# First norm of a two-block transformer kernel: x turned as it lands, roots applied behind the projections

## The reference, cut to what matters

```python
def rms_norm(x, g):
    x32 = x.astype(jnp.float32)
    y = x32 * lax.rsqrt(jnp.mean(x32 * x32, axis=-1, keepdims=True) + EPS)
    return (y * g.astype(jnp.float32)).astype(x.dtype)

h = rms_norm(x, mix_pre_g[0])
qkv = h @ w_qkv
q, k, v = jnp.split(qkv, [1024, 2048], axis=-1)
q, k = apply_partial_rope(q, cos, sin), apply_partial_rope(k, cos, sin)
# then softmax attention of two halves per head, and the rest of both blocks
```

## Time and profile before

| | |
|---|---|
| median of 3 executions | 1638.26 us (1637.98 to 1638.42) |
| span of the profiled execution, first to last instruction | 1637.0 us |
| what lies around the span (the median less the span) | 1.26 us |
| TensorE busy (matmul) | 1607.3 us, 98% |
| TensorE weight loads busy | 1406.3 us, 86% |
| VectorE busy | 1035.9 us, 63% |
| ScalarE busy | 826.8 us, 51% |
| Pool busy | 149.0 us, 9% |
| mean granted TensorE clock | 0.997 |

### The profile page before, as it was taken

One profiled execution on the slowest core, in us unless ns is written; L12 is line 12 of the kernel. 1 busy time (PEld: TensorE's weight loads), 2 busy tenths in 40 slices (PEclk: granted clock), 3 DMA queues, 4 the chain that ended last, 5 costly groups with the idle time before them and its releaser, 6 DMA issues.

```text
span 1637.0 us, 24195 instructions
## 1 busy us (share of the span) xinstructions
PE 1607.3 (98%) x10033; PEld 1406.3 (86%) x10033; DVE 1035.9 (63%) x1708; ACT 826.8 (51%) x1191; POOL 149.0 (9%) x141
## 2 busy tenths in 40 slices
PE   7999999999999999999999999999999999999997
PEld 6888888887889988888899999889888888789986
DVE  5686766655645577766665667567747876655554
ACT  4565544443669854444454564444545546354442
POOL 1220010100012200101001100001000000001000
PEclk9999999999999999999999999999999999999999
DMA  9756866777663355555555576598572564575552
GB/s 324 248 192 233 270 211 230 250 249 245 217 207 109 124 190 183 190 196 206 182 179 180 181 157 184 175 196 164 141 153 67 132 171 165 180 250 179 180 191 77
DMA packets 224412, 309.37 MB, mean 189 GB/s; under 512 B 5004, under 2 KB 146720, under 8 KB 224304
## 3 DMA queue, kind: packets, MB, share of 16 engines
q1 hardware_dynamic: 222208, 301.55, 60.2%
q0 software_dynamic: 1664, 5.84, 1.0%
q10 hardware_dynamic: 432, 0.45, 0.1%
HBM read 306.77 MB, written 1.05 MB: 188 GB/s over the span
## 4 chain that ended last, share of the span: by engine, by line
PE 89%; DVE 6%; ACT 3%; issue 1%; DMA 0%; ACTq 0%; DVEq 0%
PE ps L144 86%; PE ps L147 2%; DVE wl L157 2%; DVE SM L167 1%; DVE MT L167 1%; ACT L153 1%; ACT wh L153 1%; ACT SA L153 1%; DVE X L167 0%; ACT FT L153 0%; DVE MT L164 0%; DMA X<-in_x_dram 0%; DVE SM L163 0%; DVE SA L167 0%; ACT YF L153 0%
## 5 line engine op out<-in xcount | busy, mean ns | idle before, releaser
L157 DVE TENSOR_TENSOR wl<-raw,wh 128x1024 fp32r<-128x1024 f32 x498 | 607.8, 1260 | 381.0 <-ACT wh L153 380.3
L144 PE MATMUL ps<-XT,wh 128*128 128x256 f32 (+1 forms) x2880 | 642.2, 311 | 3.0 <-issue 2.2
L153 ACT ACTIVATE wh<-raw 128x1024 fp32r<-128x1024 f32 x498 | 501.5, 1052 | 204.6 <-PE ps L144 114.1
L144 PEld LDWEIGHTS ps<-XT,wh 128*128 128x128 f32 x2880 | 468.2, 189 | 47.3 <-issue 13.6
L144 PE MATMUL ps<-XT,wl 128*128 128x256 f32 x1792 | 502.7, 280 | 0.6 <-DVE wl L157 0.6
L144 PEld LDWEIGHTS ps<-XT,wl 128*128 128x128 f32 x1792 | 337.8, 189 | 1.3 <-DVE wl L157 1.0
L144 PE MATMUL ps<-wh,XT 128*128 128x512 f32 x704 | 224.8, 400 | 0.0
L144 PEld LDWEIGHTS ps<-wh,XT 128*128 128x128 f32 x704 | 131.3, 188 | 32.3 <-issue 1.0
L144 PE MATMUL ps<-wl,XT 128*128 128x512 f32 x352 | 139.0, 395 | 0.0
L144 PE MATMUL ps<-wh,HTH 128*128 128x512 f32 x352 | 137.4, 390 | 0.0
L144 PE MATMUL ps<-wl,HTH 128*128 128x512 f32 x352 | 137.1, 389 | 0.0
(11 more groups left out here) (293 smaller groups left out, 1740.4 us busy)
## 6 DMA issues: line engine op xcount, KB each, us to landing
raw<-in_w_ffn_in_dram SPq DMA_DIRECT2D x66, 1024.0 KB, 5.2
raw<-in_ffn_w_gate_up_dram SPq DMA_DIRECT2D x44, 1024.0 KB, 5.1
raw<-in_w_in_dram SPq DMA_DIRECT2D x40, 1024.0 KB, 8.5
raw<-in_w_ada_dram SPq DMA_DIRECT2D x36, 1024.0 KB, 5.6
raw<-in_w_ffn_out_dram SPq DMA_DIRECT2D x30, 1024.0 KB, 5.0
raw<-in_ffn_w_down_dram SPq DMA_DIRECT2D x20, 1024.0 KB, 5.0
raw<-in_a_w_qkv_dram SPq DMA_DIRECT2D x12, 1024.0 KB, 7.4
raw<-in_kv_w_dram SPq DMA_DIRECT2D x8, 1024.0 KB, 5.5
```

The lines of the kernel that those rows point to most:

```text
L144: return NOTHING if self.e is None else self.e.matmul(o, l, r, start=start, stop=stop, skip_group_check=skip)
L153: return self.e.activation(o, i, fn, bias=bias, scale=scale)
L157: return NOTHING if self.e is None else self.e.tensor_tensor(o, a, b, f)
```

## The change

- TensorE transposes x itself, as soon as x and the identity have landed, not the scaled copy OA, which is no longer made.
- On VectorE, XTL moves from step 1 to step 0, behind the first sum of squares. The roots move to step 1, and are followed by two multiplications of the identity by the roots of the two token tiles (128x128 each, tile DG).
- Before the first rotation TensorE multiplies a matrix of ones by these two diagonals (`root_row`, one float32 matmul of 256 columns): a row of roots on every partition. It takes a PSUM bank and gives it back. VectorE multiplies both tables by it, once; VectorE's and Pool's rotations wait for this.
- ScalarE evicts the first block's values with a scale per token instead of none.

```diff
@@ tensor program
+            def root_row():
+                o = take("r0")
+                pe.wait_ge(*d_cst.at())
+                pe.wait_ge(*v_small.at("r0"))
+                pe.mm(o[:, 0:T], con("one"), DG[:, 0:T], True, True).then_inc(*p_small.up("r0"))
+                give(("r0",), v_small, "turns")
             def rotate(i):
+                if i == TURNS[0]:
+                    root_row()
                 o = take("rot", i)
...
-                to_halves("h0", blocks_of(OA), lambda t, k: v_norm.at("n0", t))
+                to_halves("h0", blocks_of(X), lambda t, k: d_x.at("x"))
@@ ScalarE, rows_out(name, dst, roots=None)
+                    by = 1.0
+                    if roots is not None:
+                        act.wait_ge(*v_norm.at("n0", "r"))
+                        by = roots[:, t:t + 1]
+                    act.act(dst[:, t, n0:n0 + 512], ps(name, t, n0)[:, :], ACT.Copy, 0.0, by).then_inc(
...
-                values, tick = rows(8, rows_out("av", VA)), iter(A_TICKS)
+                values, tick = rows(8, rows_out("av", VA, small(S_MAIN + 8, 2))), iter(A_TICKS)
@@ VectorE, rotate
+                if q == 0:
+                    dve.wait_ge(*p_small.at("r0"))
+                    dve.tt(two(GB[:, 0:2 * T]), two(GB[:, 0:2 * T]), ps("r0")[:, 0:T].unsqueeze(1).to_broadcast([P, 2, T]),
+                           ALU.mult).then_inc(*v_small.up("turns"))
+                    dve.wait_ge(*v_small.at("turns"))
@@ VectorE, main
                 next_after(dve.dot(small(S_MAIN, 1), OA[:, 0, :], X[:, 0, :], X[:, 0, :]))
+                dve.wait_ge(*d_vec.at("vec"))
+                to_halves("h0", XTH, XTL, gain("mix_pre_g"))
+                yield
                 dve.wait_ge(*a_norm.at("n0", "sq"))
                 rstd(S_MAIN + 4, small(S_MAIN, 2), 2, D, ("n0", "r"))
+                dve.wait_ge(*d_id.at())
                 for t in range(2):
-                    dve.ts(OA[:, t, :], X[:, t, :], small(S_MAIN + 8 + t, 1), ALU.mult).then_inc(*v_norm.up("n0", t))
-                yield
-                dve.wait_ge(*d_vec.at("vec"))
-                to_halves("h0", XTH, XTL, gain("mix_pre_g"))
+                    m = dve.ts(DG[:, t * P:t * P + P], con("id"), small(S_MAIN + 8 + t, 1), ALU.mult)
+                m.then_inc(*v_small.up("r0"))
                 yield
@@ Pool, rotate
                 pool.wait_ge(*d_gb.at("rot"))
+                pool.wait_ge(*v_small.at("turns"))
```

More of the change, by code:

```diff
@@ L1258, in row_end, with rows_out @@
                 act.wait_ge(*(done(name, n0) if t else tile0.at(name, n0)))
-            def rows_out(name, dst):
+            def rows_out(name, dst, roots=None):
                 def evict(t, n0):
                     row_end(name, t, n0)
-                    act.act(dst[:, t, n0:n0 + 512], ps(name, t, n0)[:, :], ACT.Copy).then_inc(*a_out.up(name, t, n0))
+                    by = 1.0
[3 more added lines that the diff above has]
+                    act.act(dst[:, t, n0:n0 + 512], ps(name, t, n0)[:, :], ACT.Copy, 0.0, by).then_inc(
+                        *a_out.up(name, t, n0))
                 return evict
```

## The result

| | before | after |
|---|---|---|
| median, runs beside each other | 1638.74 us (21 runs, 20 of them 1637.34 to 1640.56) | 1641.64 us (21 runs, 1639.16 to 1643.71) |
| ratio after to before | | 1.0018, 95% interval 1.0012 to 1.0024 |
| span of the profiled execution | 1637.0 | 1641.0 |
| TensorE, VectorE, ScalarE busy | 1607.3, 1035.9, 826.8 | 1610.2, 1035.4, 826.9 |

The changed kernel is slower by 2.9 us (2.0 to 3.9 by the interval). One run of before took 3232 us, which nothing on record explains; without it the median of before is 1638.71. The spans of the two single profiles differ by 4.0.

The account below looks back on a forecast made before the run. TensorE, with 89% of the chain, was taken to bound the kernel. 1.92+1.6+0.43-0.28 = +3.7 us on a span of 1637.0 gave 1640.7, and with 1.26 around it 1641.9; 8-in-10 range 1640.0 to 1643.2.

Parts of the forecast that it names:

- the 0.2% bound: Whole kernel: about 3.3 us, or 1641.5, can be told from no change; slower than that given 0.58.
- The 1.26 around the span: Whole kernel: median 1638.26 less span 1637.0, taken as unchanged and added to the forecast span.
- Term 1: Start of the first projection: TensorE's third product waits for the weights' low halves behind XTL, +1.92 us.
- rival B: Start: weights' low halves ahead of XTL or ready in time, so TensorE starts at 13.7; -1.0 us, 1637.3, chance 0.05.
- rival A: Start: the clock is already up at 17.25, so +2.1 us, 1640.4, no change; chance 0.19.
- rival C: Low clock lasts longer, or second projection stalls: +4.7 to +5 us, 1643.1, chance 0.21.
- Term 2: Products after 17.25: TensorE at the low clock after idling, +1.6 us, bounds 0 to 2.9.
- the loss at 1438 us: Place taken as most like the new start: five groups of three took 3.22 us instead of 1.76, 1.46 lost.
- Product of roots: Between the halves of the second projection: one product of 256 float columns, +0.43 us, bounds 0.3 to 0.9.
- The covers named as hiding the rest: Second projection to first rotation: roots, later remainders, first q's eviction and table multiply hidden; 0 to +1 if any shows.
- Term 4: First paired projection, about 194 us: rotated PSUM banks remove a TensorE wait, -0.28 us, bounds -0.3 to +0.3.
- The wider spread: Whole kernel: the clock's rise differs between runs, so new runs spread more than the old kernel's 0.44 us.

Follow-up runs that it names:

- e1: Changed kernel with VectorE's remainders of weight groups 0 and 1 again ahead of the low halves of x, roots behind both: 1639.48 us, ratio 1.0003.
- e5: Changed kernel with ScalarE's high halves of x ahead of its first two weight casts: 1638.45 us, ratio 0.9996 to before.
- e7: Kernel before with one more PSUM bank taken and given back ahead of the first rotation, no product in it: one run, 1640.97 us.
- e9: Kernel before with 16 more transposes of a block of x, read by nobody, in TensorE's idle start: 1638.88 us, ratio 1.0000.
- e8: Changed kernel with the product of the roots four times in a row in the same bank: one run, 1641.78 us.
- e6: e5 with 11 more transposes to keep TensorE busy and the roots and diagonals behind the lambda sums: 1637.95 us, ratio 0.9993 to before.
- e10: The kernel of e6 timed a second time, without further edit: 1637.92 us, ratio 0.9995 to before.
- e2: Changed kernel with 34 more transposes, read by nobody, behind the first 16 to keep TensorE busy: 1640.22 us, ratio 1.0014 to before.
- e4: Changed kernel timed again with no edit: 1641.97 us, ratio 1.0023 to before.
- e3: e1 and e2 together, with 13 more transposes in place of 34 and the roots behind the lambda sums: 1637.97 us, ratio 0.9996 to before.

## Why the prediction was right

The time, 1641.9, and the measured 1641.64 agree, within the range of 1640.0 to 1643.2; the difference of medians is 2.9, forecast 3.7, and 0.18% lies just under the 0.2% bound, where I had given 0.58 to the side above it. That the totals lie 0.3 apart is in part luck: the change was forecast 0.8 too large, and the base 0.5 too small (1638.26 of three runs against 1638.74). The 1.26 around the span was no single run's either, but a median less the span of another execution; in the runs of the changed kernel it is 1.76 to 2.18. By its steps:

- *Order of the engines' queues.* Right at every station: identity 7.1 (6.90), high halves 11.95 (11.59), low halves 12.8 (12.56), remainder 16.0 (15.70), third product 17.25 (16.97). Those behind the casts are 0.24 to 0.36 early, because the first weight block landed at 9.65 and not 10.03; where the casts wait for it they start between 9.54 and 10.05 over the profiles. Term 1, +1.92, measured +1.64. e1 and e5 show it is the order: undo it on VectorE, or make the high halves early on ScalarE, and the third product is at 14.66 or 13.74. The gain of 1.0 of rival B, though, did not follow in e1, where the remainders are ahead of XTL: the third product comes 0.55 ahead of before, and the low clock behind it and the product of roots take more than that back (31.93 against 30.31).
- *The clock.* The low level at the third product came as said, and rival A is out. The longer stretch of rival C came in part: it is inside the term's bound. Term 2, +1.6, measured +2.54 in the first profile: mis-sized. I read the loss at 1438 us, where the rise came some 3 us behind the first product; here it came 3.7 to 5.3 behind the third. The bound of 2.9 held it. The forecast also put the low clock of the kernel before at little, from the one profile that paid nothing, where e7 and e9 pay about 0.6; the difference between the kernels is smaller by that in such executions.
- *Product of roots.* +0.43 forecast, 0.43 measured, three times over in e8. The covers named as hiding the rest hid it: there is no idle at the second projection, the first q is evicted at 25.11 for a rotation at 28.16, and the tables are multiplied (28.43) in VectorE's idle.
- *Banks.* Term 4, -0.28: the wait is gone in the changed kernel, but e7, and e5, e6 and e10 with it, show that the release by an earlier quarter is not enough for that. This is a right number for a reason that is not enough, and so in part luck. That a later TensorE finds the other engines ready is what the twelve profiles suggest; it was not tried by itself.
- *Where the profile's 4.0 and the medians' 2.9 part.* The profiled execution of the changed kernel itself took 1642.77, 1.1 above its median, and it had the longest of three stretches at the low clock: groups of three went over to the short pace at 22.3, 21.9 and 20.7 us in three profiles with one start. The execution of the earlier trace rows paid nothing, as said. By medians of one group the terms fit: e2, without the low clock, is 1.78 above before, near the order, the product and the wait (1.64+0.43-0.28), and e4 is 3.53 above it, though the 1.75 between them is not clear of noise.
- *The page.* The Trainium skill, "TensorE: Matmul & The Clock Gate", section "The HAM clock gate", says that the monitor runs on its own and does not start anew with the kernel. With three points of the rise for one start, the traces agree. The wider spread that I derived from it is not confirmed: the changed kernel's 21 runs spread over 4.6 us and 20 of before over 3.2, but e4's nine over 2.3 and the 31 of before beside them over 4.4. The 0.44 of the first three runs was too few to compare with.

## What to carry to other kernels

In a kernel like this, moving work earlier on one engine is worth nothing until everything between it and the bound engine moves too. Here the transposes came 4.2 us earlier; the next engine in the line had two casts in its order ahead of the new work, which waited for a weight block and ended at 11.7; and the engine after that took the new work ahead of what the bound engine needed first. Before moving a step in a hand-written order, write down for each engine what stands directly behind it and who waits for that; swapping two entries on ScalarE (e5) turned +2.9 into no loss. And price an idle stretch of TensorE twice, once for itself and once for the low clock behind it, from more than one profile: the same start paid from 1.9 us (e8) to 2.5 (after) for it.

## What the runs showed of the hardware beyond that

A stage of many small float32 products near 1226 us meets a low clock in some executions and none in others of the same order, while TensorE is busy there throughout. The distance from the transposes at 1092 to those at 1429 us is 336.96 before, 336.93 after and 336.86 in e4, and the like in e2 and e3; it is 335.6 in e1, e5, e6, e8, e9 and e10, and 338.45 in e7. The clock column for 1221 to 1240 us shows both cases, first in the profile of before, then in that of e1.

```profile
1221.00:1240.00 19.00, 19.00 (x95) 15.95 (x94) 10.77 (x32) 9.49 (x27) 0.00 (x0) 0.91 0.69 126
```

```profile
1221.00:1240.00 19.00, 18.84 (x100) 15.62 (x99) 12.07 (x33) 10.66 (x28) 0.00 (x0) 1.00 0.78 142
```

So 1.3 us, and up to 2.9, of difference between single spans follows no edit here: before has it and e9, of the same order, has not, and e4 has it and e8 has not. What decides it stays open. The profiled execution of e1, 1638.0 beside a median of 1639.48, is such a case. Small changes are to be read at landmarks of the trace or from many runs, not from one span.
